# The last block of the output, its left half finished in two pieces of 256 columns

## What is computed

```python
def rms_norm(x, g):
    y = xf * lax.rsqrt(jnp.mean(xf * xf, axis=-1, keepdims=True) + EPS)
    return (y * g.astype(jnp.float32)).astype(x.dtype)
...
def sqrelu_mlp(h, w_up, w_down):
    return jnp.square(jax.nn.relu(h @ w_up)) @ w_down
...
        h = h + sqrelu_mlp(rms_norm(h, norm_mlp_g[i]), mlp_w_up[i], mlp_w_down[i])
    return rms_norm(h, norm_final_g)
```

## Time and profile before

| | |
|---|---|
| median of 3 runs | 1169.96 us (1169.82 to 1170.15) |
| the profiled execution, its own time | 1170.25 us |
| its span in the trace | 1168.5 us |
| PE busy | 1155.5 us |
| granted TensorE clock, mean | 0.999 of full speed |

### The profile page before, as it was taken

One profiled execution on the slowest core, in us unless ns is written; L12 is line 12 of the kernel. 1 busy time (PEld: TensorE's weight loads), 2 busy tenths in 40 slices (PEclk: granted clock), 3 DMA queues, 4 the chain that ended last, 5 costly groups with the idle time before them and its releaser, 6 DMA issues.

```text
span 1168.5 us, 14805 instructions
## 1 busy us (share of the span) xinstructions
PE 1155.5 (99%) x5669; PEld 968.0 (83%) x5669; DVE 795.0 (68%) x998; ACT 558.2 (48%) x782; POOL 40.5 (3%) x88
## 2 busy tenths in 40 slices
PE   8999999999999999999999999999999999999997
PEld 7788888888888888888878998988888888888886
DVE  5647778636875856948858584494469478387587
ACT  4446667527434435435555332253454354363544
POOL 2000000000000000000020101010000000000001
PEclk9999999999999999999999999999999999999999
DMA  9347655432062161251441320205022514315202
GB/s 287 75 87 152 139 133 154 135 109 84 26 207 82 36 216 36 72 180 36 139 116 38 108 83 27 73 1 171 13 106 72 180 36 132 120 36 179 81 34 82
DMA packets 116185, 119.02 MB, mean 102 GB/s; under 512 B 38977, under 2 KB 84065, under 8 KB 116130
## 3 DMA queue, kind: packets, MB, share of 16 engines
q1 hardware_dynamic: 113328, 117.26, 33.6%
q10 hardware_dynamic: 2802, 1.00, 0.4%
HBM read 103.50 MB, written 2.10 MB: 90 GB/s over the span
## 4 chain that ended last, share of the span: by engine, by line
PE 97%; DMA 1%; DVE 1%; ACT 0%; issue 0%; SPq 0%; POOL 0%; POOLq 0%; ACTq 0%; DVEq 0%
PE bank L1049 10%; PE bank L1053 10%; PE bank L1052 10%; PE bank L1214 9%; PE bank L1218 9%; PE bank L1219 9%; PE bank L1062 6%; PE bank L1065 6%; PE bank L1066 6%; PE bank L1318 2%; PE bank L1322 2%; PE bank L1321 2%; PE bank L1488 2%; PE bank L1366 2%; PE bank L1353 1%; PE bank L1439 1%
## 5 line engine op out<-in xcount | busy, mean ns | idle before, releaser
L642 ACT ACTIVATE w_hi<-w_stage 128x2048 fp32r<-128x2048 f32 x80 | 152.0, 1912 | 148.9 <-PE bank L1214 92.4
L1695 DVE TENSOR_TENSOR w_lo<-w_stage,w_hi 128x2048 fp32r<-128x2048 f32 x88 | 200.6, 2287 | 32.3 <-ACT w_hi L642 11.9
L1049 PE MATMUL bank<-hT_lo,w_hi 128*128 128x512 f32 x512 | 199.8, 390 | 0.0
L1053 PE MATMUL bank<-hT_hi,w_lo 128*128 128x512 f32 x512 | 199.3, 389 | 0.0
L1052 PE MATMUL bank<-hT_hi,w_hi 128*128 128x512 f32 x512 | 199.2, 389 | 0.0
L1214 PE MATMUL bank<-w_lo,u_hi 128*128 128x512 f32 x336 | 131.6, 392 | 0.0
L1219 PE MATMUL bank<-w_hi,u_lo 128*128 128x512 f32 x336 | 130.8, 389 | 0.0
L1218 PE MATMUL bank<-w_hi,u_hi 128*128 128x512 f32 x336 | 130.8, 389 | 0.0
L1049 PEld LDWEIGHTS bank<-hT_lo,w_hi 128*128 128x128 f32 x512 | 96.1, 188 | 20.6 <-DVE hT_lo L1769 0.5
L1053 PEld LDWEIGHTS bank<-hT_hi,w_lo 128*128 128x128 f32 x512 | 96.1, 188 | 20.0
L1052 PEld LDWEIGHTS bank<-hT_hi,w_hi 128*128 128x128 f32 x512 | 96.1, 188 | 19.5
(11 more groups left out here) (240 smaller groups left out, 2037.1 us busy)
## 6 DMA issues: line engine op xcount, KB each, us to landing
w_stage<-in_mlp_w_up_dram SPq DMA_DIRECT2D x32, 1024.0 KB, 5.6
w_stage<-in_mlp_w_down_dram SPq DMA_DIRECT2D x32, 1024.0 KB, 5.4
w_stage<-in_fox_w_in_dram SPq DMA_DIRECT2D x36, 256.0 KB, 5.0
w_stage<-in_gla_w_in_dram SPq DMA_DIRECT2D x8, 1024.0 KB, 5.5
qa<-qk_hi SPq DMA_DIRECT2D x32, 128.0 KB
w_stage<-in_fox_w_out_dram SPq DMA_DIRECT2D x4, 1024.0 KB, 5.6
w_stage<-in_gla_w_in_dram SPq DMA_DIRECT2D x8, 512.0 KB, 5.1
w_stage<-in_gla_w_out_dram SPq DMA_DIRECT2D x4, 1024.0 KB, 5.1
```

Of the source, the lines that this page charges most:

```text
L642: act.activation(w_hi[:, HI_SLOT[unit], :], w_stage[:, STAGE[unit], :], ACT.Copy).then_inc(w_hi_made, 1)
L1049: a = pe.matmul(out, w[0][:, k, :], x[1][:, k, :], start=(k == 0), stop=False)
L1053: a = pe.matmul(out, w[1][:, k, :], x[0][:, k, :], start=False, stop=(k == KT - 1))
L1695: dve.tensor_tensor(w_lo[:, to, :], w_stage[:, at, :], fp(w_hi[:, to, :]), ALU.subtract).then_inc(w_lo_made, 1)
```

## The change

The left half of block 3 is finished in two pieces of 256 columns (`HB`). On PE, `last_block` makes piece 0 in bank 5 (columns 0 to 255) with 12 matmuls of 256 columns, then piece 1 (columns 256 to 511) in bank 7 (`END_BANK`), started afresh. What product 4 had left in columns 256 to 511 of bank 5 is therefore added to `h` ahead of time by a new DVE instruction, `end_chain`, for which PE waits. `end_collect(0)` and `end_collect(1)` add the pieces; ACT squares each, the sum of piece 0 going into `oss`, which POOL adds to `ss`. DVE multiplies piece 0 by the gain in between, and by `rstd` at the end. On PE, layer 1's last group leaves the loop and is written out.

```diff
-            sp.wait_ge(y_left, TB)
+            sp.wait_ge(end_made, 2)
...
+                    if n and t == TB - 1:
+                        pool.wait_ge(end_squared, 1)
+                        step(pool.tensor_tensor(ss[:, 1, t:t + 1], ss[:, 1, t:t + 1], oss[:, t:t + 1], ALU.add))
+                        pool.wait_ge(end_squared, 2)
+                        made = rsqrt(rstd, ss[:, 0, :], ss[:, 1, :], slice(t, t + 1))
...
-                for t in range(TB):
+                for t in range(TB - 1):
                     last_square(0, t)
                     if t == 1:
                         right(0)
                     if t:
                         right(t)
+                for part in range(2):
+                    act.wait_ge(end_added, part + 1)
+                    cols_of = slice(part * HB, (part + 1) * HB)
+                    act.activation(hn[:, TB - 1, cols_of], h[:, TB - 1, cols_of], ACT.Square,
+                                   accum_out=(oss if part == 0 else ss[:, 0, :])[:, TB - 1:TB]).then_inc(end_squared, 1)
+                right(TB - 1)
...
+                def last_block(b, part, hi, lo):
+
+                    pe.wait_ge(end_chained, 1)
+                    for cols_of in (slice(0, HB), slice(HB, S)):
+                        out = bank[b if cols_of.start == 0 else END_BANK][:, cols_of]
+                        for k in range(KT // 2):
+                            xs = [u_parts(x, k, part, part + 1)[:, P:2 * P] for x in range(2)]
+                            pe.matmul(out, xs[0], lo[:, k, cols_of], start=(k == 0 and cols_of.start > 0), stop=False,
+                                      skip_group_check=True)
+                            pe.matmul(out, xs[0], hi[:, k, cols_of], start=False, stop=False, skip_group_check=True)
+                            a = pe.matmul(out, xs[1], hi[:, k, cols_of], start=False, stop=(k == KT // 2 - 1),
+                                          skip_group_check=True)
+                        a.then_inc(sum_done, 1)
...
-                with pe.Fori(1, GROUPS if layer else GROUPS - 1) as g:
+                with pe.Fori(1, GROUPS - 1) as g:
                     wino(g)
-                if layer == 0:
-                    wino(GROUPS - 1, None, True)
+                wino(GROUPS - 1, None, True)
...
+            def end_chain():
+
+                dve.wait_ge(added, ADDS - 4)
+                to = h[:, TB - 1, HB:S]
+                dve.scalar_tensor_tensor(out=to, in0=bank[PRODUCTS[6][2] + 1][:, HB:S], scalar=mlp_scale[:, TB - 1:TB],
+                                         in1=to, op0=ALU.mult, op1=ALU.add).then_inc(end_chained, 1)
+
+            def end_collect(part):
+
+                dve.wait_ge(sum_done, ADDS + part)
+                if part:
+                    dve.wait_ge(end_chained, 1)
+                to = h[:, TB - 1, part * HB:(part + 1) * HB]
+                dve.scalar_tensor_tensor(out=to, in0=bank[END_BANK if part else PRODUCTS[6][2] + 1][:, part * HB:(part + 1) * HB],
+                                         scalar=mlp_scale[:, TB - 1:TB], in1=to, op0=ALU.mult,
+                                         op1=ALU.add).then_inc(end_added, 1)
+                dve.wait_ge(end_added, part + 1)
+                if part == 0:
+                    dve.wait_ge(end_squared, 1)
+                    dve.tensor_tensor(hn[:, TB - 1, 0:HB], to, fgain[:, 0:HB], ALU.mult).then_inc(end_scaled, 1)
+
+            def end_left():
+                dve.wait_ge(rstd_made, 2 * TB)
+                dve.scalar_tensor_tensor(out=hn[:, TB - 1, HB:S], in0=h[:, TB - 1, HB:S], scalar=rstd[:, TB - 1:TB],
+                                         in1=fgain[:, HB:S], op0=ALU.mult, op1=ALU.mult).then_inc(end_made, 1)
+                dve.wait_ge(end_scaled, 1)
+                dve.tensor_scalar(hn[:, TB - 1, 0:HB], hn[:, TB - 1, 0:HB], rstd[:, TB - 1:TB], None,
+                                  ALU.mult).then_inc(end_made, 1)
...
                     else:
+                        end_chain()
                         for t in range(TB):
                             scale_right(t)
...
-                    collect(g, 6)
+                    if not last or layer == 0:
+                        collect(g, 6)
...
                     elif last:
+                        collect(g, 6, range(1))
                         left(2)
-                        left(3)
+                        for part in range(2):
+                            end_collect(part)
+                        end_left()
```

More of the change, by code:

```diff
@@ L151 @@
 ORDER = (tuple(range(KT)), tuple(range(KT)), (4, 5, 6, 7, 0, 1, 2, 3), tuple(range(KT)))
+END_BANK = 7
 MIDDLE_BANK = (2, 3, 6, 7, 0, 1, 6, 7)
@@ L300, in fox_gla_trunk @@
             sem("rstd_made"), sem("right_scaled"), sem("y_left"), sem("y_right"))
+        end_chained, end_added, end_squared, end_scaled, end_made = (
+            sem("end_chained"), sem("end_added"), sem("end_squared"), sem("end_scaled"), sem("end_made"))
         mlp_scale_made, h_turned = sem("mlp_scale_made"), sem("h_turned")
@@ L550, in norm @@
                 for t in range(TB):
-                    if n or t < 2:
+                    if n and t == TB - 1:
[3 more added lines that the diff above has]
+                        made = rsqrt(rstd, ss[:, 0, :], ss[:, 1, :], slice(t, t + 1))
+                    elif n or t < 2:
                         pool.wait_ge(squared, n * 2 * TB + t + 1)
@@ L1195, in up, with product @@
                     tile(bank[t % 4][:], w, hT, first, t % 2 == 0).then_inc(up_done, 1)
-                def product(g, n):
+                def product(g, n, ends=False):
                     unit, part, to = PRODUCTS[n]
@@ L1213, in product @@
                         out = bank[to + t][:]
+                        if ends and t:
+                            if k == 0:
+                                last_block(to + t, part, hi, lo)
+                            continue
                         a = pe.matmul(out, xs[0], lo[:, k, :], start=(begins and k == 0), stop=False,
@@ L1235, in wino @@
                     for n in range(len(PRODUCTS)):
-                        product(g, n)
-                        if last and n == 5:
+                        product(g, n, last and layer == 1 and n == 6)
+                        if last and layer == 0 and n == 5:
                             turn_middle_right()
                 wino(0, ready_late(2 * layer + 1, adds))
-                with pe.Fori(1, GROUPS if layer else GROUPS - 1) as g:
+                with pe.Fori(1, GROUPS - 1) as g:
                     wino(g)
-                if layer == 0:
-                    wino(GROUPS - 1, None, True)
+                wino(GROUPS - 1, None, True)
             pe.wait_ge(ident_made, 1)
```

## The result

The changed kernel takes 1172.03 us (median of 20 runs, all but one of them between 1171.79 and 1172.27), the kernel before 1169.97 us (1169.80 to 1170.30, 20 runs). One run of the changed kernel took 6683.71 us and is left out of the ratio, which is 1.0017, with a 95% interval of 1.0011 to 1.0023. The change makes the kernel 2.06 us slower (2.01 without that run). That is 0.18%, inside the 0.2% that counted as the same, and on the side that was forecast.

A forecast was written before the change was run, and what follows sets the result against it. The end behind PE's last matmul was taken as bound by block 3's add and by `right(2)` after block 2's `rstd`. The chained steps put ACT's store 1.72 us later: 1169.96 + 1.72 = 1171.7 us, range 1170.9 to 1172.6.

The forecast's parts named there:

- The mechanism: End of kernel: `left(2)` delays piece 0, then DVE, ACT, DVE alternate before piece 1; the end comes 1.72 us later.
- PE: PE's block 3 matmuls: pieces ready about 1161.0 and 1162.4, off the path; PE could be 2 us late at no cost.
- The written-out group: PE's last group of layer 1: cost put at 0; rival of a code stall at its beginning, chance 0.05.
- `end_chain`: DVE at about 1152: 0.48 us, at most 0.6 with lost overlap and hand-over, but cost 0 since DVE catches up.
- DVE's queue: DVE, block 3: `left(2)` waits for `rstd` of 1162.27 ahead of piece 0; the gain's multiplication stands ahead of piece 1.
- The price of splitting: DVE's adds of block 3: 2 x 0.48 for the pieces against one of 0.75, 0.21 us more.
- the one pair that the forecast used: POOL starting behind ACT in the profile before, 1163.72 to 1163.80: a hand-over of 0.08 us.
- issue to end: From ACT's last store issue to the span's end: about 1168.5 - 1165.46 = 3.0 us before, no change added.
- The left store: DVE's end of block 3: issued between 1166.85 and 1167.35, taken as 1167.15, hidden beside ACT's; upper end adds 0.17.
- DVE's queue doesn't hold: Rival, DVE at block 3: pieces added as PE finishes, squares still behind `right(2)`; 0.23 us later, 1170.2; chance 0.04.

The follow-up runs named there:

- written_out_alone: Kernel before with only PE's last group of layer 1 written out instead of looped; 1170.03 us against 1169.94, ratio 1.0002.
- order_alone: Kernel before, nothing split, with `left(2)` moved on DVE ahead of the add of block 3; 1170.72 us, ratio 1.0007.
- gain_later: Changed kernel with the gain's multiplication of piece 0 moved behind the add of piece 1, `left(2)` still ahead; 1170.69 us, ratio 1.0007.
- both_later: Changed kernel with DVE's order piece 0, piece 1, gain's multiplication, `left(2)`; 1170.67 us, ratio 1.0007.
- gain_between: Changed kernel with `left(2)` behind both pieces on DVE and `right(2)` behind both squares on ACT, gain's multiplication between the pieces; 1170.01 us, ratio 0.9999.

## Why the prediction was right

The mechanism was the one named, and its steps can be laid beside the timeline after. Predicted and found: `left(2)` 1162.30 and 1162.27; the add of piece 0 1162.97 and 1162.94; the first square 1163.49 and 1163.45; the gain's multiplication 1164.07 and 1164.06; the add of piece 1 1164.42 and 1164.42; the second square 1164.94 and 1164.93; POOL 1165.52 and 1165.58; ACT's store 1167.18 and 1167.23.

- **PE.** A matmul of 256 columns each 0.12 us, the last at 1162.01 (near 1162.0 was forecast), off the path. The written-out group costs nothing (written_out_alone).
- **`end_chain`.** It runs at 1152.08 for 0.48 us, and DVE has caught up behind it, as `left(0)` shows, which started at 1157.40 against 1157.44 in the earlier trace rows:

```profile
1152.08 0.48 DVE L1785 SCALAR_TENSOR_TENSOR h<-bank,columns_of,h 128x256 f32<-128x256 f32 x1
...
1157.40 0.74 DVE L1778 SCALAR_TENSOR_TENSOR hn<-h,rstd,w_stage 128x512 f32<-128x512 f32 x1
```

- **DVE's queue.** This is the term that the forecast called decisive, and experiments show it: order_alone and gain_later take the 1.81 apart into 0.75 and 1.07.
- **The price of splitting.** The add measured 0.47 and 0.48 us, so the row gave the right term, and not the 0.39 us estimated from the table of the Trainium skill's page VectorE: DVE Perf Modes, section on the TRN2 errata. In the change both adds stand on the path, one behind the other, and the 0.21 us for the pieces' fixed part is paid. That splitting always costs it is not so: gain_later and order_alone are level. In gain_later's trace the two adds run from 1162.83 to 1163.70 and the first square starts at 1163.34, so the second add lies beside it.
- **The size.** 1.72 was forecast, 2.06 measured. Up to ACT's last issue the traces have 1.81. The largest part of the 0.09 more is POOL: it started 0.14 us behind the accumulator's read (1165.44 to 1165.58), where the one pair that the forecast used had 0.08. The kernels with the extra addition into `ss` show 0.14 to 0.15, those without it 0.07 to 0.08. In the former POOL waits for its own step as well as for ACT; that this wait is the cause was not tried apart. And from issue to end it took 3.17 instead of 3.04, which the forecast took as fixed. Together that is 1.94 in the traces; the rest, 0.12, lies between traces and medians, and 0.05 of it is the run of 6683.71 us, which is in the median of 20.
- **The left store.** The forecast had it at 1167.15, hidden beside ACT's. It was issued at 1167.27, 0.04 behind ACT's, the only trace of these in which it is the last: DVE started 0.09 us behind POOL, at 1166.49 instead of 1166.37, and took until 1167.24. This explains 0.04 of the 0.13 between 3.17 and 3.04; the other 0.09 is about the spread of this length (3.01 to 3.09) among the kernels that leave block 2's store no later than before.
- **The rival "DVE's queue doesn't hold".** Its mechanism is right in that ACT's `right(2)` is the next stop and no gain is to be had by DVE's order alone. Its number, 1170.2, was too low: both_later took 1170.67, since `left(2)` then lies beside POOL's addition.

## What to carry to other kernels

Work for an older block that waits for something late must not stand ahead of the newest block's work in an in-order queue; look up when its release comes, not where it seems to belong. Where a last step is cut into pieces, nothing between the pieces should wait for another engine while the next piece is ready; the same small multiplication cost 1.07 us where it stood in the path and next to nothing where the next piece was still being computed. Behind the point where the order is mended, the next bounds stand close together, here ACT's queue, POOL against DVE, and the store of the block before, and each took back most of what the last had given. No kernel here is faster than the one before by more than the measurement can tell.

## What the runs showed of the hardware

- POOL's 0.19 us addition took 0.48, 0.71 and 0.47 us when it started while DVE was in an operation with two inputs in SBUF, and ended 0.05 us behind DVE's end. In gain_between it started 0.10 us before the end of such an operation and took 0.19. Beside one with an input in PSUM it took 0.19.
- When the store before the last ones is issued matters at the end of a kernel too: with block 2's store 0.35 us later (gain_between, 4.76 behind PE's first matmul against 4.41) and ACT's last one 0.25 us earlier, the span went on for 3.28 us behind the last issue instead of 3.04, though nothing more was stored; the transfers ran at some 400 GB/s.
